# Modulation units of the head, all tiles on TensorE in four groups of 32 columns

## What is computed

```python
cond = jax.nn.silu(c)                                  # (1, 2048)
for layer in range(DEPTH):
    mod = cond @ w_ada[layer] + b_ada[layer]           # 2048 x 12288 matrix per layer
    sh_m, sc_m, g_m, sh_f, sc_f, g_f = jnp.split(mod[:, None, :], N_MOD, axis=-1)
    h = rms_norm(x, norm_mix_gain[layer]) * (1.0 + sc_m) + sh_m
    y = pool_mixer(h, ...) if layer % 2 == 0 else hgrn2_mixer(h, ...)
    x = x + g_m * y
    h = rms_norm(x, norm_ffn_gain[layer]) * (1.0 + sc_f) + sh_f
    x = x + g_f * swiglu(h, w_ffn_in[layer], w_ffn_out[layer])
return rms_norm(x, final_gain)
```

## Time and profile before

| what | value |
|---|---|
| median of 3 runs | 2167.86 us (2167.64 to 2169.1) |
| profiled execution, its span | 2165.9 us |
| TensorE busy (matmul) | 2130.7 us, 98% |
| VectorE, ScalarE busy | 1640.7 us (76%), 998.1 us (46%) |
| first FFN product (L646) starts | 177.16 us |

### The profile page before, as it was taken

How to read it: one execution, slowest core, us unless ns; L and a number is a source line. 1 busy time by engine, 2 the same in 40 slices (tenths; PEclk the granted TensorE clock), 3 DMA queues, 4 the chain that set the end, 5 groups by cost and what they waited for, 6 DMA issues and landing times.

```text
span 2165.9 us, 24699 instructions
## 1 busy us (share of the span) xinstructions
PE 2130.7 (98%) x9533; PEld 1722.3 (80%) x9533; DVE 1640.7 (76%) x1693; ACT 998.1 (46%) x1117; POOL 22.4 (1%) x89
## 2 busy tenths in 40 slices
PE   7999999999999999999999999999999999999998
PEld 3557887888888888888888888878888888888886
DVE  5779998899988887779787887677755666456645
ACT  2324544444444434465555465544454444444344
POOL 1000000000000000020000000000000000000000
PEclk9999999999999999999999999999999999999999
DMA  9999997899999998756656654678855556568664
GB/s 383 419 418 348 359 331 267 298 321 337 319 354 330 342 340 289 254 200 237 210 198 216 222 196 163 193 276 296 284 185 188 186 181 193 186 193 295 239 214 146
DMA packets 149249, 574.34 MB, mean 265 GB/s; under 512 B 16678, under 2 KB 16870, under 8 KB 141452
## 3 DMA queue, kind: packets, MB, share of 16 engines
q1 hardware_dynamic: 149132, 572.77, 74.8%
HBM read 570.60 MB, written 2.10 MB: 264 GB/s over the span
## 4 chain that ended last, share of the span: by engine, by line
PE 93%; DVE 3%; DMA 2%; ACT 1%; issue 1%; SPq 0%; DVEq 0%; ACTq 0%
PE prod L646 28%; PE prod L650 28%; PE prod L647 28%; PE modp L676 2%; DVE acc L1396 2%; PE small L723 1%; DMA ada<-in_ada_sections 1%; PE small L908 1%; DMA ada_head<-in_ada_sections 1%; PE modp L683 1%; PE small L883 0%; PE modp L712 0%; DVE w_lo L1347 0%; PE prod L620 0%; PE prod L619 0%
## 5 line engine op out<-in xcount | busy, mean ns | idle before, releaser
L994 ACT ACTIVATE w_hi<-raw 128x1024 fp32r<-128x1024 f32 x696 | 736.3, 1061 | 975.9 <-PE prod L650 842.3
L1347 DVE TENSOR_TENSOR w_lo<-raw,w_hi 128x1024 fp32r<-128x1024 f32 x696 | 848.9, 1223 | 413.3 <-ACT w_hi L994 411.2
L646 PE MATMUL prod<-w_hi,h_hi 128*128 128x512 f32 x2072 | 817.2, 394 | 2.8 <-DVE part_gate L1746 1.1
L650 PE MATMUL prod<-w_hi,h_lo 128*128 128x512 f32 x2072 | 807.1, 390 | 0.0
L647 PE MATMUL prod<-w_lo,h_hi 128*128 128x512 f32 x2072 | 806.7, 389 | 0.0
L646 PEld LDWEIGHTS prod<-w_hi,h_hi 128*128 128x128 f32 x2072 | 389.1, 188 | 85.5 <-issue 2.9
L650 PEld LDWEIGHTS prod<-w_hi,h_lo 128*128 128x128 f32 x2072 | 388.9, 188 | 82.1 <-DVE h_lo L1505 0.3
L647 PEld LDWEIGHTS prod<-w_lo,h_hi 128*128 128x128 f32 x2072 | 389.3, 188 | 78.5 <-issue 1.0
L1396 DVE SCALAR_TENSOR_TENSOR acc<-ada,cond,acc 128x1024 f32<-128x1024 f32 x255 | 326.4, 1280 | 1.1 <-DMA ada<-in_ada_mixed 0.3
L646 PE MATMUL prod<-w_hi,g_hi 128*128 128x512 f32 x680 | 265.7, 391 | 0.0
L650 PE MATMUL prod<-w_hi,g_lo 128*128 128x512 f32 x680 | 264.6, 389 | 0.0
(11 more groups left out here) (207 smaller groups left out, 1082.5 us busy)
## 6 DMA issues: line engine op xcount, KB each, us to landing
raw<-in_w_ffn_in SPq DMA_DIRECT2D x352, 512.0 KB, 4.7
ada<-in_ada_sections SPq DMA_DIRECT2D x256, 512.0 KB, 6.1
raw<-in_w_ffn_out SPq DMA_DIRECT2D x176, 512.0 KB, 4.2
raw<-in_hgrn_w_in SPq DMA_DIRECT2D x128, 512.0 KB, 3.6
ada_head<-in_ada_sections SPq DMA_DIRECT2D x36, 1024.0 KB, 15.6
raw<-in_hgrn_w_out SPq DMA_DIRECT2D x32, 512.0 KB, 3.5
ada<-in_ada_sections SPq DMA_DIRECT2D x12, 1024.0 KB, 11.9
ada<-in_ada_mixed SPq DMA_DIRECT2D x16, 512.0 KB, 8.7
```

What stands on the lines that cost most here:

```text
L646: pe.matmul(o, hi[:, k, ts], wh, start=(begin and s == 0), stop=False)
L650: mm = pe.matmul(o, lo[:, k, ts], wh, start=False, stop=(end and s == n - 1))
L994: act.activation(w_hi[:, slot], raw[:, r], ACT.Copy).then_inc(hi_ready, 1)
L1347: dve.tensor_tensor(w_lo[:, slot], raw[:, r], w_hi[:, slot], ALU.subtract).then_inc(lo_ready, 1)
```

## The change

All 16 tiles of a unit of the head go to TensorE. `cond_rows` is now 32 columns wide per tile: zero, except that column 0 holds `cond`. Four tiles make a group; tile `part` of it is multiplied into the rows 32 `part` to 32 `part` + 31 of `modp`, so in the order of the program four matmuls that follow each other write four different groups of rows, first for the left 512 columns, then for the right. Rows 0, 32, 64 and 96 of `modp` end up with a quarter of the sum each, and the others with zero. ScalarE copies `modp` to `acc` or `feat_acc` (`take_rows`, semaphore `rows_taken`), and from there the columns are summed as before; a gate's bias is added by VectorE in `head_bias`, and its `reduce_unit` begins with start=True. VectorE folds nothing in the head. On TensorE pool products 0 and 1 move ahead of the third pooled block and of unit 3, and products 2 and 3 ahead of unit 5; on SP one unit's load moves behind pool_w and pool_scale.

```diff
-    PE_LOADS = [7, 7, 7, 6, 8, 8, 9]
+    GROUPS = 4
+    GROUP = P // GROUPS
...
-            cond_rows = sb("cond_rows", [P, max(PE_LOADS), P], where=pooling)
+            cond_rows = sb("cond_rows", [P, KD, GROUP], where=pooling)
...
+            pool.memset(cond_rows[:, :, :], 0.0).then_inc(rows_begun, 1)
...
             def multiply_loads(u):
+
                 pe.wait_ge(unit_taken, u)
-                n_rows, _ = folded(u)
-                for k in range(n_rows):
-                    n = u * KD + k
-                    slot, _ = ada_slot(n)
-                    ada_arrived(pe, n)
+                for first in range(0, KD, GROUPS):
                     for o in range(2):
-                        mm = pe.matmul(modp[:, o], cond_rows[:, k], ada_buffer(slot)[:, o * CH:(o + 1) * CH], start=(k == 0),
-                                       stop=(in_columns(u) and k == n_rows - 1))
-                    mm.then_inc(ada_free[slot], 1)
+                        for k in range(first, first + GROUPS):
+                            n, part = u * KD + k, k - first
+                            slot, _ = ada_slot(n)
+                            if o == 0:
+                                ada_arrived(pe, n)
+                            mm = pe.matmul(modp[part * GROUP:(part + 1) * GROUP, o], cond_rows[:, k],
+                                           ada_buffer(slot)[:, o * CH:(o + 1) * CH],
+                                           start=(first == 0), stop=(first == KD - GROUPS))
+                            if o:
+                                mm.then_inc(ada_free[slot], 1)
...
             def head_columns(u):
 
-                pe.wait_ge(row_added, columns_before(u) + 1)
+                pe.wait_ge(rows_taken, u + 1)
...
             multiply_loads(2)
             head_columns(2)
+            pool_product(0)
+            pool_product(1)
+            pooled(3)
             multiply_loads(3)
-            pooled(3)
-            pool_product(0)
             head_columns(3)
             multiply_loads(4)
-            pool_product(1)
             reduce_unit(4)
-            multiply_loads(5)
             pool_product(2)
             pool_product(3)
+            multiply_loads(5)
             reduce_unit(5)
             multiply_loads(6)
...
-            for k in range(max(PE_LOADS)):
-                rows_k = act.activation(cond_rows[:, k], ones[:, :], ACT.Identity, bias=zero[:, 0:1], scale=cond[:, k:k + 1])
-            rows_k.then_inc(rows_ready, 1)
+            act.wait_ge(rows_begun, 1)
+            act.activation(cond_rows[:, :, 0], cond[:, :], ACT.Copy).then_inc(rows_ready, 1)
             t.tick("small0")
+
+            def take_rows(u):
+
+                ada_used(act, u * KD + KD - 1)
+                if buffer_uses(u) > 0:
+                    act.wait_ge(unit_reduced, buffer_uses(u))
+                act.activation(unit_buffer(u), modp[:, :, :].rearrange("p a n -> p (a n)"), ACT.Copy).then_inc(rows_taken, 1)
+
+            take_rows(0)
             take_unit(0)
...
+            def head_bias(u):
+                dve.wait_ge(rows_taken, u + 1)
+                add_bias(u)
```

More of the change, by code:

```diff
@@ L707, in reduce_unit @@
                 pe.wait_ge(unit_summed, 2 * (rows_before(u) + 1))
-                a, begun = unit_buffer(u), u < len(HEAD)
-                if not begun:
-                    pe.wait_ge(unit_taken, u)
+                a = unit_buffer(u)
+                pe.wait_ge(unit_taken, u)
                 for o in range(2):
-                    mm = pe.matmul(modp[:, o], ones[:, :], a[:, o * CH:(o + 1) * CH], start=not begun, stop=True)
+                    mm = pe.matmul(modp[:, o], ones[:, :], a[:, o * CH:(o + 1) * CH], start=True, stop=True)
                 mm.then_inc(unit_reduced, 1)
@@ L1126, in _ @@
             pooled(1)
+            take_rows(1)
             take_unit(1)
-            hi()
-            hi()
+            take_rows(2)
             take_unit(2)
+            for _ in range(HG):
+                hi()
             act.wait_ge(gain_ready, 2)
@@ L1133, in _ @@
             pooled(3)
-            hi()
-            hi()
+            take_rows(3)
             take_unit(3)
-            take_unit(4)
             for _ in range(HG):
                 hi()
+            take_rows(4)
+            take_unit(4)
             square_updated(0)
             square_updated(1)
+            take_rows(5)
             take_unit(5)
@@ L1147, in _ @@
             root()
+            take_rows(6)
             take_unit(6)
@@ L1374, in fold @@
             def fold():
-                u = t.get("unit")
-                first, last = folded(u)
-                k = first + t.get("folds")
+                u, k = t.get("unit"), t.get("folds")
                 n = u * KD + k
@@ L1380, in fold @@
                 a = unit_buffer(u)
-                if k == first and u > 0 and turned(u - 1):
+                if k == 0 and turned(u - 1):
                     dve.wait_ge(parts_ready, turned_before(u))
-                elif k == first and buffer_uses(u) > 0:
+                elif k == 0:
                     dve.wait_ge(unit_reduced, buffer_uses(u))
                 ada_arrived(dve, n)
-                if in_columns(u) and k == last - 1:
-                    ada_used(dve, n - 1)
-                    ada_used(dve, u * KD + first - 1)
-                    row = a[0:1, :].rearrange("p (a n) -> p a n", a=2)
-                    dve.tensor_tensor(row, row, modp[0:1, :, :], ALU.add).then_inc(row_added, 1)
-                    dve.wait_ge(row_added, columns_before(u) + 1)
-                if k == first:
+                if k == 0:
                     ins = dve.tensor_scalar(a, ada_buffer(slot), cond[:, k:k + 1], None, ALU.mult)
@@ L1398, in fold, with add_bias @@
                 t.tick("folds")
-                if k == last - 1:
-                    if not in_columns(u):
-                        ada_used(dve, n)
-                        at = rows_before(u)
-                        dve.wait_ge(bias_loaded[at % 2], 32 * (at // 2 + 1))
-                        for r in range(2):
-                            row = 64 * (at % 2) + 32 * r
-                            b = a[row:row + 1, r * CH:(r + 1) * CH]
-                            dve.tensor_tensor(b, b, bias[row:row + 1, :], ALU.add).then_inc(unit_summed, 1)
+                if k == KD - 1:
+                    ada_used(dve, n)
+                    add_bias(u)
                     t.tick("unit")
                     t.n["folds"] = 0
+            def add_bias(u):
+                a, at = unit_buffer(u), rows_before(u)
+                dve.wait_ge(bias_loaded[at % 2], 32 * (at // 2 + 1))
+                for r in range(2):
+                    row = 64 * (at % 2) + 32 * r
+                    b = a[row:row + 1, r * CH:(r + 1) * CH]
+                    dve.tensor_tensor(b, b, bias[row:row + 1, :], ALU.add).then_inc(unit_summed, 1)
+            def head_bias(u):
+                dve.wait_ge(rows_taken, u + 1)
+                add_bias(u)
             def turn_columns(u):
@@ L1433, in take_columns @@
                 ins.then_inc(unit_taken, 1)
-            def folds(n):
-                for _ in range(n):
-                    fold()
             def norm_root():
```

36 lines of the change are left out of this document (10 added, 26 removed).

## The result

The changed kernel takes **2175.94 us** (median of 8 runs, 2172.34 to 2178.09), the kernel before on the same chip 2168.97 us (8 runs, 2167.59 to 2170.8): a ratio of 1.0032, interval 1.0022 to 1.0041. It is slower by 7.0 us. Forecast was no change, 2167.5. The profiled execution took 2175.8 us, its span is 2174.0.

What follows compares the result with a forecast made beforehand. The head was taken as bound by its data stream, then 6 us between data and columns. Tail 2.2 us shorter, unit 6 1.8 us late: net -0.4, 2167.5 us, no change; range 2164 to 2188.

Steps and rivals of the forecast that it cites:

- Four at once: Head multiplications on TensorE: four tiles on separate columns run together, 1.72 us a group and 6.9 us a unit.
- the rivals of two and none at once: Head multiplications: two, 13.7 us a unit, 2184 us (0.31 with weight-load bound); none, 27.5 us, 2268 us (0.05).
- a unit bound by weight loads: Head multiplications: 64 weight loads of 0.19 us make 12.2 us a unit, 2177 us; chance 0.31 together with two at once.
- The stream: DMA in the head: 0.414 MB/us, the last pair of unit 6 landing at 167.8 us if asked for in time.
- The end: From unit 6 landed at 169.6 us through last group, copy and sums to the first FFN product at 176.8.
- the request for unit 6: SP's load after unit 5's first group at 146.6 us; first pair lands at 151.9, 1.8 us late against 150.1.
- The slots of units 1 to 5 come free in time: Buffer slots in the head: unit 3's first group frees unit 4's by 97 us where 102 would do.
- From the gate's reduce to the end of VectorE's tok were 152.01 to 157.00, 5.0 us: Gate 4, behind unit 4's bias: 5.0 us taken from the old trace, ending at 134.0 us.
- The 48 matmuls of the two products, 0.228 us each: Pool products 2 and 3 on TensorE ahead of unit 5's multiplication, ending at 144.9 us.
- No clock below 1 between 126 and 150 us: Sign for the main case: TensorE's granted clock stays full around gate 4 and pool products 2 and 3.
- if the DMA share breaks before 100 us: Sign that the forecast is wrong: the head's data stream drops before 100 us.
- The rival "the clock falls": Gate 4: a falling clock slows products 2 and 3 by 3 to 5 us, 2171 to 2173 us; chance 0.11.

Runs made afterwards that it cites:

- e3: Changed kernel with thrown-away filler matmuls in TensorE's quiet stretches and pool products 2 and 3 behind unit 5's multiplication: 2166.80 us, 0.9991 of the kernel before.
- e5: e3 with gate 5 reduced between pool products 2 and 3 instead of behind product 3: 2165.96 us, 0.9987 of the kernel before.
- e1: Changed kernel with thrown-away filler matmuls around the columns of units 1 and 2 and the sum of gate 4: 2170.04 us, 1.0003 of the kernel before.
- e7: Changed kernel with filler matmuls at gate 4 alone, three ahead of its reduction and three behind: 2173.29 us, 1.0019 of the kernel before.
- e2: Changed kernel with pool products 2 and 3 back behind unit 5's multiplication, no filler: 2169.97 us, 1.0005 of the kernel before.
- e8: Changed kernel with all pool products and the units' loads back in the order of before, no filler: 2171.27 us, 1.0009 of the kernel before.
- e10: e8 with filler matmuls at units 1 and 2 alone: 2169.26 us, 0.9998 of the kernel before.
- e11: e9 with filler matmuls at units 1 and 2 and gate 5 reduced between products 2 and 3: 2166.88 us, 0.9987 of the kernel before.
- e9: e8 with the units' loads where the changed kernel has them in SP's queue: 2171.17 us, 1.0008 of the kernel before.
- e4: Changed kernel with a group's four tiles on the same 32 columns and the groups on different ones: 2249.03 us (one run).
- e6: Kernel before the change with the filler matmuls of e1 at the same places: 2176.77 us, 1.0035 of the kernel before.

## Why the prediction was wrong

**Four at once: right.** 7.07 us a unit against the 6.9 reckoned; the rivals of two and none at once are out. The Trainium skill's page "TensorEngine Tiling (Array Packing)", section "Key Properties", has tiles that load and multiply in parallel, and the trace agrees. By my reading of the Trainium skill's page "TensorE: Matmul & The Clock Gate", Part 3, section "The mechanism", the two records of each matmul, in strict order, would have held a unit to 13.7 us; the measured 7.07 decides against that reading. That 2175.94 us lies inside the range (2164 to 2188), and near the 2177 of a unit bound by weight loads, is luck: the range reached there for two at once, and neither happened, since the weight loads of four matmuls take 0.13 us together.

**The stream: right.** With no hole, unit 6's last group starts at 167.23 (e3) and 167.28 (e5); 167.8 was reckoned. **The row's copy: right**, 1.02 us. **The end: right**: from unit 6's last pair to the first product 7.2 us were reckoned, and 177.37 to 184.80 is 7.4.

**The failed step is the request for unit 6**, of which the prediction said "That is 1.8 us late". The mechanism, a late request that empties the stream, was right, and its size was wrong: 155.00, where 146.6 was reckoned. Two things were put at nothing, the lateness of earlier requests and a fall of the clock. Term by term:

- "The slots of units 1 to 5 come free in time" failed. Unit 3 was asked for at 75.39 and unit 4 at 105.08, "where 102 would do"; products 0 and 1 ran from 86.48 to 100.3, not "from about 81 to 92". Unit 4's last group ended at 130.8 in place of 126.4: 4.4 us, mostly the first two holes (1.7 + 2.3). I had reckoned from landings alone, as if TensorE took each group when it had landed. In the kernel before VectorE took tiles beside TensorE, and slots came free early; now every slot waits for TensorE's turn.
- "From the gate's reduce to the end of VectorE's tok were 152.01 to 157.00, 5.0 us" was read at the full clock; the reduce took 3.68 in place of 1.88: 1.8 us.
- "The 48 matmuls of the two products, 0.228 us each" were read at the full clock too: 140.30 to 152.98 is 12.7 in place of 10.9: 1.8 us.
- First group of unit 5, 2.0 in place of 1.7: 0.3.

Together 8.3 of 8.4 us. Of the signs, "No clock below 1 between 126 and 150 us" failed: the windows show 0.64 and 0.72. And a sign of being wrong came, "if the DMA share breaks before 100 us": the slice at 75 to 80 us moves 279 GB/s.

**The rival "the clock falls"** had the mechanism at gate 4, for 3 to 5 us and a chance of 0.11; there the fall cost 3.6 us by the two terms above. "The quiet before the fall at 31 us was longer than these gaps" spoke against it: that was one fall, taken for a limit. The other fall of the earlier trace rows, from 79 us on, says otherwise. TensorE of the kernel before it:

```profile
76.42 0.39 PE L694 MATMUL modp<-ident,brows 64*128 64x8 f32 x2 [1.79 <-DVE acc L1390]
77.74 2.77 PE L683 MATMUL modp<-ones,acc 128*128 128x1 f32 x16 [0.94 <-DVE acc L1396]
```

Its gaps, 1.79 and 0.94 us, are shorter than the 2.5 and 3.2 reckoned at gate 4. The falls at 65 and 84 us I didn't look for. That the falls cost time is shown by e1 and e7: with the gaps filled the gate's sum is back at 1.95 us and the requests come sooner. They were several, and they came on top of a request that was late anyway; priced alone, at one place, none of them makes 7 us.

One fall more is chance. Unit 1's last group took, in the changed kernel,

```profile
51.72 3.52 PE L675 MATMUL modp<-ada_head,cond_rows 128*32 128x512 f32 x12 [1.43 <-DMA ada_head<-in_ada_sections]
```

and 3.50 and 3.58 us in e1 and e2, but 1.91 in e3, e5, e8, e10 and e11 (in e7 and e9 the fall came a group earlier), though TensorE's program is the same up to there. It moves the request for unit 3 by 1 to 1.6 us (74.11 to 74.28 in e7, e8 and e9, which have no filler there either), so part of the first hole differs from execution to execution.

What stays open: how the first two holes share out between order and clock in the changed kernel itself. e8 keeps one hole with the order undone, e10 closes it with filler (with the luck told above), e9 all but closes it with the queue, so no single cause can be named. ScalarE's later splits, which hold products 0 and 1 for 2.56 us ahead of unit 4's request, were not varied.

## What to carry to other kernels

When an edit makes an engine that frees buffers faster, but also makes it the only one that frees them, follow each request in the program's order (engine free, group done, slot free, request, landing), not from the landings. Then ask how long that engine now sits quiet ahead of work on the path, and price the work behind at both clock levels. Work that frees a buffer belongs ahead of work that has time; here that order, a few thrown-away multiplications in real slack and gate 5's sum one product sooner turned 0.32% lost into 0.13% gained (e5).

## What the runs showed of the hardware

Four fp32 matmuls of 128x32 weights by 512 columns on four groups of columns run side by side in the time of one, 64 records in 7.07 us; in e4, on the same columns, 64 took 24.2 us. TensorE's weight loads in the changed kernel's unit 3 come four at a time, 0.43 us apart, and four of 32 columns take 0.13 us where one of 128 took 0.19:

```profile
103.49 0.13 PEld L675 LDWEIGHTS modp<-ada,cond_rows 128*32 128x32 f32 x4 [0.30 <-issue]
103.92 0.13 PEld L675 LDWEIGHTS modp<-ada,cond_rows 128*32 128x32 f32 x4 [0.30 <-issue]
```

And the same thrown-away multiplications made one kernel faster by 5.9 us, where TensorE was idle, and the other slower by 7.7, where it was not (e1, e6).
